# Residual additions merged into the phase that reads their result, chunk by chunk

## The chip, the core and the metric

The kernel runs on one core of one Trainium2 chip. The metric is the device time of one execution in microseconds (us). The core's engines work side by side and meet only at semaphores: PE multiplies matrices (PEld loads its weights), DVE is the vector engine, ACT the scalar engine with its activation functions, POOL a second, slower vector engine, and SP issues most of the DMAs. PE, DVE, ACT and POOL compute on SBUF, PE writes to PSUM.

## The reference

One layer of a hybrid decoder, for 1024 prompt tokens and 8 x 4 sample tokens together (1056 tokens). Cut to what the change touches:

```python
def _rmsnorm(x, g):
    y = x * lax.rsqrt(jnp.mean(x * x, axis=-1, keepdims=True) + NORM_EPS)
    return y * g

f = _swiglu(_rmsnorm(h, ffn1_pre_g), ffn1_wg, ffn1_wu, ffn1_wd)
h = h + 0.5 * _rmsnorm(f, ffn1_post_g)            # r1
u = _rmsnorm(h, mix_pre_g) @ w_in                 # input projection
...                                               # attention, RWKV-7, gates: not touched
h = h + _rmsnorm(mix @ w_out, mix_post_g)         # r2
f = _swiglu(_rmsnorm(h, ffn2_pre_g), ffn2_wg, ffn2_wu, ffn2_wd)
h = h + 0.5 * _rmsnorm(f, ffn2_post_g)            # r3
gp = sigmoid(_rmsnorm(h, ple_pre_g) @ w_ple_gate)
h = h + _rmsnorm(gp * (pemb @ w_ple_proj), ple_post_g)   # r4
```

D_MODEL is 1024, FFN_DIM 2816, everything is float32.

## The kernel before

The stream `x` lies in SBUF channel by channel: 8 chunks (KC) of 128 channels by 1056 tokens (T). PE works on three token blocks of 352 (TB, NTB = 3). The layer is a row of phases, and no engine starts a phase before all have ended the last one: f1 (first feed-forward), r1 (its residual), in (input projection), the middle, merge, r2, f2, r3, pl (per-layer embedding), r4.

**Products.** Each is made of three matmuls on split operands (`mm3`): a float32 value is written as a rounded part `hi` and a rest `lo`. ACT makes `hi`, DVE makes `lo`, for weights and stream alike. A unit is 128 output channels: 8 chunks x 3 blocks x 3 = 72 matmuls. Units of weights come by DMA from the SP queue. A phase begins with `gain_split` (u_hi on ACT, u_lo on DVE, with the first weights between the second and third chunk), and PE's first block of the first unit takes chunk after chunk as u_lo comes (`u_lo_ready`).

**Norms.** The factor 1/rms of a token is applied when a product leaves PSUM. `Norm` makes it in a long chain: ACT squares the chunks, DVE adds them up (`dve_sums`), PE sums over channels with 9 one-column matmuls (`pe_sums`), ACT takes the root, DVE makes the reciprocal (128x9) and a diagonal matrix (`dve_diag`), PE spreads it to all partitions (`pe_spread`), and ACT copies it to `rb` (`act_rb`). In f1, f2 and in, PE does this behind the first or second unit. `NextNorm` takes the squares of a phase's output while its last products run, for the residual behind it (not for r2, which squares for itself).

**Residuals.** `residual_phase` loads all 8 chunks of the old stream in one DMA of 4.2 MB (L699), scales each chunk on DVE out of PSUM (L730), adds the old chunk (L719; even chunks on POOL, odd ones on DVE) and stores the new stream with 8 DMAs. Only then the next phase begins.

**Order.** There is no scheduler: each engine runs its list in the order of the code. Names: `c_x` is x, `f_psg`, `f_psu`, `f_psd` the PSUM tiles of a feed-forward, `in_ps` and `pl_ps` those of in and pl, `n_*` the tiles of a norm, `r_*` of a residual.

Of the kernel before, what the change touches and what calls it, by code (L numbers as in the profile page):

```python
# [213 lines left out]
def gain_split(nc, act, dve, x, g, hi, lo, hi_ready, lo_ready, first_weights, x_in=None):  # L214


    for c in range(x.shape[1]):
        if c == 2:
            first_weights()
        if x_in is not None:  # L220
            x_in(act or dve, c)
        if act is not None:
            act.activation(hi[:, c, :], x[:, c, :], ACT.Copy, scale=g[:, c:c + 1]).then_inc(hi_ready, 1)
        if dve is not None:
            dve.wait_ge(hi_ready, c + 1)
            dve.scalar_tensor_tensor(out=lo[:, c, :], in0=x[:, c, :], scalar=g[:, c:c + 1],
                                     in1=hi[:, c, :], op0=ALU.mult, op1=ALU.subtract).then_inc(lo_ready, 1)


def ffn_phase(nc, env, name, x, g_col, wgu, wd, buf, x_src=None, reading=None):  # L230
# [7 lines left out]
    with Phase(nc) as ctx:  # L238
# [10 lines left out]
        norm = Norm(nc, ctx, name + "n", env, KC, D_MODEL, buf)  # L249
        after = NextNorm(nc, ctx, name, buf)  # L250
        gate, up = norm.sq[:, 0, :], norm.sq[:, 1, :]
# [54 lines left out]
        def x_in(eng, c):  # L306
            if x_src is not None:
                eng.wait_ge(x_loaded[c], 16)

        @block.sync  # L310
        def _(sp):
# [6 lines left out]
            load(0, 0, 0)  # L318
            if x_src is not None:
                for c in range(KC):  # L320
                    sp.dma_start(x[:, c, :], x_src[:, c, :]).then_inc(x_loaded[c], 16)

            def step(s, sv):
                for u in units(s)[1 if sv == 0 else 0:]:
                    load(s, sv, u)
# [14 lines left out]
        def _(act):  # L340
            gain_split(nc, act, None, x, g_col, u_hi, u_lo, u_hi_ready, u_lo_ready,
                       lambda: split_hi(act, 0, 0), x_in)
            norm.act_squares(act, x)
# [11 lines left out]
            def step(s, sv):  # L355
                if sv < NS:
                    for u in (1, 2, 3):
                        split_hi(act, s, u)
# [28 lines left out]
        def _(dve):  # L387
            gain_split(nc, None, dve, x, g_col, u_hi, u_lo, u_hi_ready, u_lo_ready,
                       lambda: split_lo(dve, 0, 0), x_in)
            norm.dve_sums(dve)  # L390
            norm.dve_diag(dve)
            rb3 = norm.rb[:, :].rearrange("p (b t) -> p b t", b=NTB)
# [37 lines left out]
            def step(s, sv):  # L430
                has_up = sv < NS
                last_up = isinstance(s, int) and s == NS - 1
                if has_up:
                    split_lo(dve, s, 1)
                    split_lo(dve, s, 2)
                    gate_evac(s, 0)
                    split_lo(dve, s, 3)
# [14 lines left out]
                if sv > 0:  # L452
                    wait(dve, added, (s - 1) * 24)
                    if sv == 1:
                        dve.wait_ge(u_lo_ready, KC)
                        dve.wait_ge(norm.sq_ready, KC)
                        if reading is not None:
                            dve.wait_ge(*reading)
# [17 lines left out]
        @block.gpsimd  # L476
        def _(pool):
            after.add(pool, range(1, KC - 1))

        @block.tensor  # L480
        def _(pe):
            def up_unit(s, u):
# [3 lines left out]
                for b in range(NTB):  # L486
                    for c in range(KC):
                        if isinstance(s, int) and s == 0 and u == 0 and b == 0:
                            pe.wait_ge(u_lo_ready, c + 1)
# [6 lines left out]
            def step(s, sv):  # L496
                if sv < NS:
                    for u in range(4):
                        up_unit(s, u)
                        if sv == 0 and u == 0:  # L500
                            norm.pe_sums(pe, ps_d[:, 1, :])
                            norm.pe_spread(pe, nbanks)
# [18 lines left out]
class Units:  # L521
# [39 lines left out]
    def product(self, pe, out, k, first, chunks, x_hi, x_lo, tokens, x_ready=None):  # L561


        for c in range(chunks):
            if x_ready is not None:
                pe.wait_ge(x_ready, c + 1)
# [6 lines left out]
def token_block(b):  # L573
    return slice(b * TB, (b + 1) * TB)


def input_projection_phase(nc, env, x, g_col, w_units, proj, buf, reading):


    with Phase(nc) as ctx:  # L580
# [8 lines left out]
        norm = Norm(nc, ctx, "inn", env, KC, D_MODEL, buf)  # L589
# [10 lines left out]
        def _(sp):  # L600
# [5 lines left out]
            for k in range(2):  # L606
                wu.load(sp, 0, k)
            with sp.Fori(1, N_IN // 2) as i:
# [7 lines left out]
            sp.wait_ge(*reading)  # L616

        @block.scalar
        def _(act):
            gain_split(nc, act, None, x, g_col, u_hi, u_lo, u_hi_ready, u_lo_ready,  # L620
                       lambda: wu.split_hi(act, 0, 0))
            wu.split_hi(act, 0, 1)
            norm.act_squares(act, x)
# [7 lines left out]
        def _(dve):  # L631
            gain_split(nc, None, dve, x, g_col, u_hi, u_lo, u_hi_ready, u_lo_ready,
                       lambda: wu.split_lo(dve, 0, 0))
            wu.split_lo(dve, 0, 1)
            norm.dve_sums(dve)
            norm.dve_diag(dve)
            dve.wait_ge(norm.rb_ready, 3)

            def evac(i, k):
# [3 lines left out]
                                  norm.rb[:, :].rearrange("p (b t) -> p b t", b=NTB), ALU.mult)\  # L643
# [14 lines left out]
        def _(pe):  # L658
            def unit(i, k):
                wu.ready(pe, i, k)  # L660
                wait(pe, unit_out, i * 2 + (k - 1))
                for b in range(NTB):
                    mm = wu.product(pe, ps[:, k, b, 0:TB], k, 0, KC, u_hi, u_lo, token_block(b),
                                    u_lo_ready if isinstance(i, int) and i == 0 and k == 0 and b == 0 else None)
                mm.then_inc(wu.used, 1)

            unit(0, 0)
            unit(0, 1)
            norm.pe_sums(pe, psn[:, 1, :])
# [2113 lines left out]
```

## Time and profile before

| what | value |
|---|---|
| median of 3 runs | 3861.78 us (3854.52 to 3871.53) |
| profiled execution: its time | 3863.07 us |
| its span in the profile | 3861.3 us |
| PE busy | 3430.6 us (89%) |
| DVE busy | 1695.9 us (44%) |
| ACT busy | 929.8 us (24%) |
| POOL busy | 440.8 us (11%) |
| granted TensorE clock, mean | 0.932 of 2.4 GHz |

Busy time is time in which an engine has an instruction in work, so 89% of PE does not say that the last 11% is all there is to win; what the engines wait for at the seams between phases is read from the timeline.

### The profile page before, as it was taken

The numbers are of one execution on the slowest core, as the hardware profiler recorded it, in microseconds if no ns is written. First come the engines' busy times: TensorE is split into PE (matmuls) and PEld (weight loads), VectorE is DVE, ScalarE is ACT, GpSimd is POOL, SyncE is SP. The second block draws the span as 40 slices with busy tenths as digits, with TensorE's granted clock in tenths as the row PEclk, the third lists the DMA queues.
The fourth block names the chain that finished last, engine by engine and source line by source line (L and its number), as shares of the span: only waits on it lengthen the run. The fifth ranks groups of instructions, "written<-read, shape, count | busy, mean of one in ns | idle before, by whom it ended". The sixth has DMA issues, their size and how long they took to land. (4 is left out here: it accounts for less than half of the span.)

```text
span 3861.3 us, 69674 instructions
## 1 busy us (share of the span) xinstructions
PE 3430.6 (89%) x28907; PEld 3086.5 (80%) x28907; DVE 1695.9 (44%) x2998; ACT 929.8 (24%) x1610; POOL 440.8 (11%) x457
## 2 busy tenths in 40 slices
PE   7999999969999799889994888869869999999776
PEld 6999999959999637766662767659859999999766
DVE  3343343353121245345444777755154443343443
ACT  3111111121000105434441333333221111111131
POOL 0000000020000000033331344420010000000212
PEclk9999999979999898989996899979979999999878
DMA  2011111122222300056552011023121111111122
GB/s 102 34 55 45 50 39 45 44 107 75 91 94 94 110 2 13 16 206 208 191 192 60 14 31 31 12 95 117 67 83 50 50 50 33 50 50 39 75 80 97
DMA packets 114583, 279.64 MB, mean 72 GB/s; under 512 B 45428, under 2 KB 56500, under 8 KB 113236
## 3 DMA queue, kind: packets, MB, share of 16 engines
q1 hardware_dynamic: 95860, 199.87, 15.4%
q0 software_dynamic: 18432, 75.51, 5.6%
q8 instruction: 229, 3.75, 0.4%
q14 instruction: 62, 0.51, 0.0%
HBM read 231.41 MB, written 43.80 MB: 71 GB/s over the span
## 5 line engine op out<-in xcount | busy, mean ns | idle before, releaser
L79 PE MATMUL f_psg<-f_u_hi,f_w_hi 128*128 128x352 f32 x1056 | 347.1, 329 | 62.7 <-DVE f_w_lo L336 58.2
L428 DVE TENSOR_TENSOR c_x<-c_x,f_psd 128x352 f32<-128x352 f32 x480 | 246.2, 519 | 318.0 <-PE f_psd L81 318.0
L79 PE MATMUL f_psd<-f_hid_hi,f_w_hi 128*128 128x352 f32 x1056 | 350.3, 332 | 18.2 <-DVE c_x L428 9.8
L332 ACT ACTIVATE f_w_hi<-f_raw 128x1024 fp32r<-128x1024 f32 x132 | 136.6, 1054 | 915.7 <-PE f_psd L81 352.3
L79 PE MATMUL f_psu<-f_u_hi,f_w_hi 128*128 128x352 f32 x1056 | 342.5, 324 | 5.5 <-DVE f_w_lo L336 5.5
L80 PE MATMUL f_psg<-f_u_lo,f_w_hi 128*128 128x352 f32 x1056 | 342.7, 325 | 0.0
L81 PE MATMUL f_psg<-f_u_hi,f_w_lo 128*128 128x352 f32 x1056 | 342.5, 324 | 0.0
L80 PE MATMUL f_psd<-f_hid_lo,f_w_hi 128*128 128x352 f32 x1056 | 341.6, 324 | 0.0
L81 PE MATMUL f_psd<-f_hid_hi,f_w_lo 128*128 128x352 f32 x1056 | 341.3, 323 | 0.0
L80 PE MATMUL f_psu<-f_u_lo,f_w_hi 128*128 128x352 f32 x1056 | 340.2, 322 | 0.0
L81 PE MATMUL f_psu<-f_u_hi,f_w_lo 128*128 128x352 f32 x1056 | 339.8, 322 | 0.0
L336 DVE TENSOR_TENSOR f_w_lo<-f_raw,f_w_hi 128x1024 fp32r<-128x1024 f32 x132 | 159.2, 1221 | 353.0 <-ACT f_w_hi L332 353.0
L79 PE MATMUL in_ps<-in_u_hi,inw_hi 128*128 128x352 f32 x864 | 281.5, 326 | 31.3 <-DVE inw_lo L555 30.1
L80 PE MATMUL in_ps<-in_u_lo,inw_hi 128*128 128x352 f32 x864 | 278.8, 323 | 0.0
L81 PE MATMUL in_ps<-in_u_hi,inw_lo 128*128 128x352 f32 x864 | 278.5, 322 | 0.0
L79 PEld LDWEIGHTS f_psg<-f_u_hi,f_w_hi 128*128 128x128 f32 x1056 | 201.5, 191 | 67.5 <-DVE f_w_lo L336 45.6
L118 POOL TENSOR_TENSOR n_total<-n_total,n_sq 128x1056 f32<-128x1056 f32 x18 | 44.4, 2469 | 1735.7 <-ACT n_sq L111 1735.7
L79 PEld LDWEIGHTS f_psd<-f_hid_hi,f_w_hi 128*128 128x128 f32 x1056 | 199.6, 189 | 35.1 <-DVE c_x L428 20.2
L79 PEld LDWEIGHTS f_psu<-f_u_hi,f_w_hi 128*128 128x128 f32 x1056 | 199.5, 189 | 5.8 <-DVE f_w_lo L336 5.8
L80 PEld LDWEIGHTS f_psg<-f_u_lo,f_w_hi 128*128 128x128 f32 x1056 | 202.0, 191 | 0.0
L81 PEld LDWEIGHTS f_psg<-f_u_hi,f_w_lo 128*128 128x128 f32 x1056 | 201.6, 191 | 0.0
L80 PEld LDWEIGHTS f_psd<-f_hid_lo,f_w_hi 128*128 128x128 f32 x1056 | 200.0, 189 | 0.0
(391 smaller groups left out, 7226.3 us busy)
## 6 DMA issues: line engine op xcount, KB each, us to landing
f_raw<-in_ffn_gu SPq DMA_DIRECT2D x88, 512.0 KB, 4.3
f_raw<-in_ffn_d SPq DMA_DIRECT2D x44, 512.0 KB, 4.0
proj<-in_out SPq DMA_DIRECT2D x36, 528.0 KB, 2.9
inw_raw<-in_w_in_units SPq DMA_DIRECT2D x36, 512.0 KB, 3.9
h<-c_x SPq DMA_DIRECT2D x24, 528.0 KB, 2.7
r_old<-h SPq DMA_DIRECT2D x3, 4224.0 KB, 12.9
c_x<-proj SPq DMA_DIRECT2D x16, 528.0 KB, 4.5
mgw_raw<-in_merge_units SPq DMA_DIRECT2D x16, 512.0 KB, 4.7
```

The costliest lines, as they stand in the source:

```text
L79: pe.matmul(out, w_hi, x_hi, start=start, stop=False)
L80: pe.matmul(out, w_hi, x_lo, start=False, stop=False)
L81: return pe.matmul(out, w_lo, x_hi, start=False, stop=stop)
L118: eng.tensor_tensor(total, total, self.buf.sq[:, c % 2, :], ALU.add).then_inc(self.added, 1)
L332: act.activation(w_hi[:, u % 3, :], raw[:, u % 3, :], ACT.Copy).then_inc(hi_done, 1)
L336: dve.tensor_tensor(w_lo[:, u % 3, :], raw[:, u % 3, :], w_hi[:, u % 3, :], ALU.subtract).then_inc(lo_done, 1)
L428: dve.tensor_tensor(a, a, ps_d[:, n % 2, 0:TB], ALU.add).then_inc(added, 1)
```

## The change

The phases r1, r2 and r3 are gone. Their work is done at the head of in, f2 and pl by a class `Residual`; r4 stays as a phase of its own. `Residual` keeps a ring of three old chunks instead of all eight, loads and stores chunk by chunk, and DVE scales chunk c+1 before it splits chunk c. DVE adds chunks 0, 2, 4, 6, 7 and POOL 1, 3, 5 (in pl DVE adds 0, 1, 2, 4, 6, 7). `WideNorm` takes the place of `Norm` in these phases: PE sums the squares of a chunk straight into three rows of PSUM, 32 partitions each, the root and the reciprocal work on 96x352, and a matmul with one row spreads each block. At the head of in, f1, f2 and pl PE takes each chunk for all three blocks at once, the sum of the chunk's squares behind it; the second unit (except in pl) is done in blocks behind the first, and the spread comes behind the second. In pl the products of the embedding come ahead of the chunks.

```diff
+class WideNorm:
+    def act_square(self, act, x, c):
+        wait(act, self.sq_summed, c - 1)
+        act.activation(self.buf.sq[:, c % 2, :], x[:, c, :], ACT.Square).then_inc(self.sq_ready, 1)
+    def pe_sum(self, pe, bank, c):
+        pe.wait_ge(self.sq_ready, c + 1)
+        for b in range(NTB):
+            mm = pe.matmul(bank[32 * b:32 * (b + 1), 0:TB], self.env.ones[:, 0:32],
+                           self.buf.sq[:, c % 2, token_block(b)], start=c == 0, stop=c == KC - 1)
+        mm.then_inc(self.sq_summed, 1)
...
+    def dve_reciprocal(self, dve):
+        dve.wait_ge(self.sd_ready, 1)
+        dve.reciprocal(self.buf.rs[0:self.ROWS, :], self.buf.sd[0:self.ROWS, :]).then_inc(self.rs_ready, 1)
+    def pe_spread(self, pe, banks):
+        pe.wait_ge(self.rs_ready, 1)
+        for b in range(NTB):
+            if b >= len(banks):
+                pe.wait_ge(self.rb_ready, b - len(banks) + 1)
+            pe.matmul(banks[b % len(banks)][:, 0:TB], self.env.ones[32 * b:32 * b + 1, :],
+                      self.buf.rs[32 * b:32 * b + 1, :], start=True, stop=True).then_inc(self.spread, 1)
...
+class Residual:
+    RING = 3
+    def sp_all(self, sp):
+        for c in range(self.RING):
+            self.sp_load(sp, c)
+        for c in range(KC):
+            self.sp_store(sp, c)
+            if c + self.RING < KC:
+                self.sp_load(sp, c + self.RING)
+    def dve_scale(self, dve, c, rb):
+        dve.scalar_tensor_tensor(out=self.x[:, c, :], in0=self.x[:, c, :], scalar=self.gain[:, c:c + 1], in1=rb,
+                                 op0=ALU.mult, op1=ALU.mult).then_inc(self.scaled, 1)
+        if c in self.by_dve:
+            self.add_old(dve, c, self.dve_added)
...
@@ input projection
+            res_norm.act_root(act, psn[:, 1, :])
+            res_norm.act_rb(act, nbanks)
+            wu.split_hi(act, 0, 0)
+            for c in range(KC):
+                res.wait_chunk(act, c)
+                act_hi(act, x, g_col, u_hi, c, u_hi_ready)
+                if c == 0:
+                    wu.split_hi(act, 0, 1)
+                norm.act_square(act, x, c)
...
+            for c in range(KC):
+                pe.wait_ge(u_lo_ready, c + 1)
+                if c == KC - 1:
+                    norm.pe_sum(pe, psn[:, 1, :], c)
+                if c == 0:
+                    wu.ready(pe, 0, 0)
+                for b in range(NTB):
+                    mm = mm3(pe, ps[:, 0, b, 0:TB], ...)
+                if c < KC - 1:
+                    norm.pe_sum(pe, psn[:, 1, :], c)
             unit(0, 1)
-            norm.pe_sums(pe, psn[:, 1, :])
             norm.pe_spread(pe, nbanks)
```

DVE at the seam from f1 to the input projection, before: the residual r1 (`r1_*`), and behind the two branches the input projection's own splits (`in_u_lo`, weights `inw_lo`) and norm (`n1_*`).

```order
L723 TENSOR_SCALAR r1_gain<-c_gains 128x8
L177 RECIPROCAL n1_rs<-n1_sd 128x9
L182 TENSOR_TENSOR n1_diag<-c_ident,n1_rs 128x512 x2
L182 TENSOR_TENSOR n1_diag<-c_ident,n1_rs 128x128
L730 SCALAR_TENSOR_TENSOR c_x1<-c_x1,r1_gain,r1_rb 128x1056 x3
L719 TENSOR_TENSOR c_x1<-c_x1,r1_old 128x1056
L730 SCALAR_TENSOR_TENSOR c_x1<-c_x1,r1_gain,r1_rb 128x1056 x2
```

The same place with the change (`inr_*` is the residual inside the input projection):

```order
L327 TENSOR_SCALAR inr_gain<-c_gains 128x8
L268 RECIPROCAL n1_rs<-n1_sd 96x352
L332 SCALAR_TENSOR_TENSOR c_x1<-c_x1,inr_gain,n1_rb 128x1056
L340 TENSOR_TENSOR c_x1<-c_x1,inr_old 128x1056
L741 TENSOR_TENSOR inw_lo<-inw_raw,inw_hi 128x1024
L332 SCALAR_TENSOR_TENSOR c_x1<-c_x1,inr_gain,n1_rb 128x1056
L359 SCALAR_TENSOR_TENSOR in_u_lo<-c_x1,c_gains,in_u_hi 128x1056
L741 TENSOR_TENSOR inw_lo<-inw_raw,inw_hi 128x1024
L332 SCALAR_TENSOR_TENSOR c_x1<-c_x1,inr_gain,n1_rb 128x1056
L340 TENSOR_TENSOR c_x1<-c_x1,inr_old 128x1056
L359 SCALAR_TENSOR_TENSOR in_u_lo<-c_x1,c_gains,in_u_hi 128x1056
```

The splits of the stream stand between the scalings now; the scaling reads its factor from the SBUF tile `n1_rb`, where it read the PSUM tile `r1_rb`; and the diagonal is gone.

PE at the same seam with the change, from the head of the phase (before, 9 one-column matmuls and a spread of 512, 512 and 32 columns stood in r1, and 72 matmuls of the first unit, block by block, at the head of the input projection):

```order
L257 MATMUL in_psn<-n1_total,c_ones 32x352 x3
L276 MATMUL in_psn<-n1_rs,c_ones 128x352 x3
L79 MATMUL in_ps<-in_u_hi,inw_hi 128x352
L80 MATMUL in_ps<-in_u_lo,inw_hi 128x352
L81 MATMUL in_ps<-in_u_hi,inw_lo 128x352
L79 MATMUL in_ps<-in_u_hi,inw_hi 128x352
L80 MATMUL in_ps<-in_u_lo,inw_hi 128x352
L81 MATMUL in_ps<-in_u_hi,inw_lo 128x352
L79 MATMUL in_ps<-in_u_hi,inw_hi 128x352
L80 MATMUL in_ps<-in_u_lo,inw_hi 128x352
L81 MATMUL in_ps<-in_u_hi,inw_lo 128x352
L251 MATMUL in_psn<-n1_sq,c_ones 32x352 x3
```

Nine matmuls and three sums now stand for each chunk, eight times over.

## Rows read from the trace of the kernel before

**Rows 1.** The page's first line: span of the profiled execution

```profile
span 3861.3 us, 69674 instructions
```

**Rows 2.** Timeline of PE, head of f1: start, duration, instruction, idle before and releaser

```profile
43.89 0.66 PE L79 MATMUL f_psu<-f_u_hi,f_w_hi 128*128 128x352 f32 x1 [2.71 <-DVE f_w_lo L336]
```

**Rows 3.** Timeline of DVE, head of f1: the second unit has ended

```profile
57.98 1.26 DVE L407 TENSOR_TENSOR n_sq<-f_psu,n_rb 128x1056 f32<-128x1056 f32 x1 [10.71 <-PE f_psu L81]
```

**Rows 4.** Timeline of PE, r1 and head of the input projection

```profile
827.37 3.97 PE L166 MATMUL r_sum<-c_ones,n_total 128*128 128x1 f32 x18 [3.79 <-PEq L62]
832.68 4.05 PE L206 MATMUL r_rb<-n_diag,c_ones 128*128 128x512 f32 x6 [1.34 <-DVE n_diag L182]
...
900.14 0.66 PE L79 MATMUL in_ps<-in_u_hi,inw_hi 128*128 128x352 f32 x1 [3.01 <-DVE inw_lo L555]
```

**Rows 5.** Timeline of DVE, r1

```profile
840.23 3.76 DVE L730 SCALAR_TENSOR_TENSOR c_x<-c_x,r_gain,r_rb 128x1056 f32<-128x1056 f32 x3 [6.80 <-DMA r_old<-in_x]
```

**Rows 6.** The tile r_old: from issue to landing

```profile
DMA to landing us min/median/max: 12.6/12.8/13.0
```

**Rows 7.** Costliest groups of the page: busy us, mean ns of one

```profile
L332 ACT ACTIVATE f_w_hi<-f_raw 128x1024 fp32r<-128x1024 f32 x132 | 136.6, 1054 | 915.7 <-PE f_psd L81 352.3
...
L336 DVE TENSOR_TENSOR f_w_lo<-f_raw,f_w_hi 128x1024 fp32r<-128x1024 f32 x132 | 159.2, 1221 | 353.0 <-ACT f_w_hi L332 353.0
```

**Rows 8.** The tile c_x: min/median/max ns of its instructions

```profile
L148 ACT ACTIVATE n_sq<-c_x x35: 1066/1084/1094, 22.7 to 3701.0; 128x1056 f32<-128x1056 f32 x35
L730 DVE SCALAR_TENSOR_TENSOR c_x<-c_x,r_gain,r_rb x32: 1296/1302/1315, 840.2 to 3854.1; 128x1056 f32<-128x1056 f32 x32
...
L830 ACT ACTIVATE c_x<-mg_pso x24: 464/465/466, 2696.7 to 2784.4; 128x352 f32<-128x352 f32 x24
...
L223 ACT ACTIVATE f_u_hi<-c_x,c_gains x16: 1159/1161/1177, 11.5 to 2833.9; 128x1056 fp32r<-128x1056 f32 x16
...
L719 POOL TENSOR_TENSOR c_x<-c_x,r_old x16: 2419/3367/3439, 841.7 to 3853.1; 128x1056 f32<-128x1056 f32 x16
L719 DVE TENSOR_TENSOR c_x<-c_x,r_old x16: 1241/1281/2136, 843.9 to 3855.4; 128x1056 f32<-128x1056 f32 x16
```

**Rows 9.** The tile pl_u_lo, min/median/max ns

```profile
L226 DVE SCALAR_TENSOR_TENSOR pl_u_lo<-c_x,c_gains,pl_u_hi x8: 1305/1306/4752, 3674.3 to 3693.0; 128x1056 fp32r<-128x1056 f32 x8
```

**Rows 10.** Timeline of POOL, head of pl

```profile
3682.40 4.65 POOL L977 TENSOR_TENSOR pl_p_lo<-pl_p,pl_p_hi 128x2112 fp32r<-128x2112 f32 x1 [11.71 <-ACT pl_p_hi L931]
```

**Rows 11.** Timeline of PE in the sample attention: four column strips

```profile
1803.16 0.64 PE L1728 MATMUL sa_ps_o<-sa_pages,sa_weights 128*32 128x256 f32 x8
```

**Rows 12.** The tile n_rs, min/median/max ns

```profile
L177 DVE RECIPROCAL n_rs<-n_sd x8: 215/215/215, 36.1 to 3833.2; 128x9 f32<-128x9 f32 x8
```

**Rows 13.** The line L1314, min/median/max ns

```profile
L1314 DVE RECIPROCAL pa_rinv<-pa_rsum x8: 191/192/203, 1463.0 to 1625.2; 128x8 f32<-128x8 f32 x8
```

**Rows 14.** Windows of f1: busy us (instructions) by engine, granted clock, DMA share, GB/s

```profile
24.00:28.00 4.00, 3.98 (x25) 3.98 (x26) 3.71 (x4) 2.97 (x4) 0.00 (x0) 1.00 0.00 0
...
44.00:48.00 4.00, 4.00 (x14) 4.00 (x15) 3.27 (x3) 2.84 (x3) 0.00 (x0) 0.50 0.00 0
```

**Rows 15.** Timeline of ACT, head of f1: the first chunk is in

```profile
11.51 1.17 ACT L223 ACTIVATE f_u_hi<-c_x,c_gains 128x1056 fp32r<-128x1056 f32 x1 [3.63 <-DMA c_x<-in_x]
```

**Rows 16.** Timeline of ACT, start of r2

```profile
2785.67 1.08 ACT L145 ACTIVATE n_total<-c_x 128x1056 f32<-128x1056 f32 x1 [0.77 <-PEq L62]
```

**Rows 17.** Timeline of DVE, head of f2: the second unit has ended

```profile
2871.27 1.26 DVE L407 TENSOR_TENSOR n_sq<-f_psu,n_rb 128x1056 f32<-128x1056 f32 x1 [9.96 <-PE f_psu L81]
```

**Rows 18.** Timeline of PE, start of r3

```profile
3643.22 3.95 PE L166 MATMUL r_sum<-c_ones,n_total 128*128 128x1 f32 x18 [3.96 <-PEq L62]
```

**Rows 19.** Timeline of DVE in pl: the first unit's last block has ended

```profile
3723.79 0.52 DVE L967 TENSOR_TENSOR pl_gate<-pl_ps,n_rb 128x352 f32<-128x352 f32 x1 [3.19 <-PE pl_ps L81]
```

**Rows 20.** Timeline of PE, start of r4

```profile
3828.86 3.97 PE L166 MATMUL r_sum<-c_ones,n_total 128*128 128x1 f32 x18 [4.93 <-PEq L62]
```

**Rows 21.** Timeline of DVE, r4

```profile
3841.95 3.76 DVE L730 SCALAR_TENSOR_TENSOR c_x<-c_x,r_gain,r_rb 128x1056 f32<-128x1056 f32 x3 [7.04 <-DMA r_old<-h]
```

More of the change, by code:

```diff
@@ L387, in _ @@
         def _(dve):
[L388 to L392, printed above, removed]
+            if res is not None:
+                res.dve_gain(dve)
+                res_norm.dve_reciprocal(dve)
+                dve.wait_ge(res_norm.rb_ready, NTB)
+                res.dve_scale(dve, 0, buf.rb[:, :])
+            split_lo(dve, 0, 0)
+            for c in range(KC):
+                if res is not None and c < KC - 1:
+                    res.dve_scale(dve, c + 1, buf.rb[:, :])
+                x_in(dve, c)
+                dve_lo(dve, x, g_col, u_hi, u_lo, c, u_hi_ready, u_lo_ready)
+                if c == 0:
+                    split_lo(dve, 0, 1)
+            norm.dve_reciprocal(dve)
+            rb3 = buf.rb[:, :].rearrange("p (b t) -> p b t", b=NTB)
             def gate_evac(s, j):
@@ L477, in _ @@
         def _(pool):
+            if res is not None:
+                res.pool_adds(pool)
             after.add(pool, range(1, KC - 1))
@@ L559, in ready, with product @@
         pe.wait_ge(self.lo_done, i * 2 + (k + 1))
-    def product(self, pe, out, k, first, chunks, x_hi, x_lo, tokens, x_ready=None):
+    def product(self, pe, out, k, first, chunks, x_hi, x_lo, tokens):
         for c in range(chunks):
-            if x_ready is not None:
-                pe.wait_ge(x_ready, c + 1)
             w = slice((first + c) * P, (first + c + 1) * P)
@@ L607, in _ @@
                 wu.load(sp, 0, k)
+            res.sp_all(sp)
             with sp.Fori(1, N_IN // 2) as i:
@@ L615, in _ @@
                 sp.wait_ge(stored[k], 16 * (N_IN // 2))
-            sp.wait_ge(*reading)
+            sp.wait_ge(res.stored, 16 * KC)
+        @block.gpsimd
+        def _(pool):
+            res.pool_adds(pool)
         @block.scalar
         def _(act):
[L620 to L623, printed above, removed]
+            res_norm.act_root(act, psn[:, 1, :])
+            res_norm.act_rb(act, nbanks)
+            wu.split_hi(act, 0, 0)
+            for c in range(KC):
+                res.wait_chunk(act, c)
+                act_hi(act, x, g_col, u_hi, c, u_hi_ready)
+                if c == 0:
+                    wu.split_hi(act, 0, 1)
+                norm.act_square(act, x, c)
             norm.act_root(act, psn[:, 1, :])
@@ L631, in _ @@
         def _(dve):
[L632 to L637, printed above, removed]
+            res.dve_gain(dve)
+            res_norm.dve_reciprocal(dve)
+            dve.wait_ge(res_norm.rb_ready, NTB)
+            res.dve_scale(dve, 0, buf.rb[:, :])
+            wu.split_lo(dve, 0, 0)
+            for c in range(KC):
+                if c < KC - 1:
+                    res.dve_scale(dve, c + 1, buf.rb[:, :])
+                res.wait_chunk(dve, c)
+                dve_lo(dve, x, g_col, u_hi, u_lo, c, u_hi_ready, u_lo_ready)
+                if c == 0:
+                    wu.split_lo(dve, 0, 1)
+            norm.dve_reciprocal(dve)
+            dve.wait_ge(norm.rb_ready, NTB)
             def evac(i, k):
@@ L981, in _ @@
         def _(pe):
-            for n in range(KC):
+            res_norm.pe_total(pe, psn[:, 1, :])
+            res_norm.pe_spread(pe, nbanks)
+            wu.ready(pe, 0, 0)
+            pe.wait_ge(p_lo_ready, 1)
+            for b in range(NTB):
+                wu.product(pe, ps[:, b, 1, 0:TB], 0, KC, PC, p_hi, p_lo, token_block(b))
+            for c in range(KC):
+                pe.wait_ge(u_lo_ready, c + 1)
+                if c == KC - 1:
+                    norm.pe_sum(pe, psn[:, 1, :], c)
+                w = slice(c * P, (c + 1) * P)
+                for b in range(NTB):
+                    mm = mm3(pe, ps[:, b, 0, 0:TB], wu.hi[:, 0, w], wu.lo[:, 0, w], u_hi[:, c, token_block(b)],
+                             u_lo[:, c, token_block(b)], c == 0, c == KC - 1)
+                    if c == KC - 1:
+                        mm.then_inc(wu.used, 1)
+                if c < KC - 1:
+                    norm.pe_sum(pe, psn[:, 1, :], c)
+            norm.pe_spread(pe, nbanks)
+            for n in range(1, KC):
                 wu.ready(pe, n // 2, n % 2)
```

298 lines of the change are left out of this document (202 added, 96 removed).

## The prediction, made before the changed kernel ran

> **What bounds the kernel now.** I read the page, then the timeline of each engine at the seams between phases, then single tiles. The span is 3861.3 us [rows 1] and PE is busy through most of it, so a change at the seams can win only what PE waits or idles there; the loops between are untouched. At four seams PE waits for a chain through the other engines. I mark each by two points: its start, and the first moment at which PE goes on with work that the change leaves as it is.
>
> | seam | start | point behind it | length |
> |---|---|---|---|
> | f1 | first chunk in, 11.5 [rows 15] | second unit ended, 57.9 [rows 3] | 46.4 |
> | r1 and in | 827.4 | third unit starts, 900.1 [rows 4] | 72.7 |
> | r2 and f2 | 2785.7 [rows 16] | second unit ended, 2871.2 [rows 17] | 85.5 |
> | r3 and pl | 3643.2 [rows 18] | first unit ended, 3723.7 [rows 19] | 80.5 |
> | r4 | 3828.9 [rows 20] | the end, 3861.3 [rows 1] | 32.4 |
>
> In r1 the scaling starts 12.9 us after the phase, because it waits 6.8 us for the DMA of the old stream [rows 5], which takes 12.8 us to land [rows 6]; r4 shows the same wait of 7.0 us [rows 21].
>
> **Prices.** Behind one another, DVE's operations on 128x1056 follow at 1.25 us each (three in 3.76 [rows 5]), be it scaling, adding or splitting; a weight split costs ACT 1.05 and DVE 1.22 [rows 7]. ACT needs 1.16 for u_hi and 1.08 for a square, 0.47 for 352 columns out of PSUM [rows 8]. A product matmul takes 0.16 us at the high level of the clock (25 in 3.98) and 0.29 at the low one (14 in 4.00) [rows 14]: nine of them 1.4 or 2.6, a whole unit of 72 11.5 us.
>
> The sum of squares has no row. Eight plain float32 matmul instructions of 256 columns in four strips of 32 took 0.64 us in all [rows 11]; with 352 columns that makes 0.9 us for a chunk's three strips, or 1.8 at the low clock. That the strips run side by side is the assumption; one behind the other, three blocks are 1056 plain columns, and 1056 such columns took 4.05 us at the low clock [rows 4], so 2.0 at the high one. I take 0.9. The spread is bounded by the same row: 4.05 for all, 1.35 a block at the low clock. The third block waits for a free bank, so I take first block, copy, third block, copy: 3.9 us at the low clock, 3.0 at the high.
>
> The reciprocal on 352 columns has no row either. Nine columns take 215 ns [rows 12] and eight 191 [rows 13]. Below, it costs per column what the scaling does, 352 of 1056 columns in 1.3 us [rows 8], 0.4 us; above, 24 ns for each further column, the difference of the two rows, makes 8.5 us. The upper end also takes the whole 191 ns of eight columns as their own, with no fixed part, which no engine here shows. So I sit near the lower end: 1.5.
>
> **The port that DVE and POOL share.** This decides the feed. DVE's additions took up to 2136 ns where 1241 is the least; POOL's took 3367 in the median where 2419 is the least [rows 8]. A split of pl took 4752 ns instead of 1306 [rows 9], just while POOL held a 4.65 us operation [rows 10]. But the scaling, which reads its factor from PSUM, never took over 1315 next to POOL [rows 8]. So a DVE instruction with two SBUF operands and a POOL one exclude each other, for a whole instruction. The change moves the factor of the scaling to SBUF, so that now every DVE operation of the feed is of this kind, and POOL's time adds to DVE's instead of hiding.
>
> The Trainium skill says so too ("SBUF — State Buffer", "SBUF: two separate sides"): the pair is an exclusive lock, held for the whole instruction, against a DVE instruction with two SBUF inputs. By that rule the trace agrees; if the two only shared, each feed would be some 7 us shorter and the sum 22 us larger.
>
> **The feed of in and f2.** DVE has 8 scalings, 5 additions, 8 splits and 2 weight splits, 21 x 1.25 + 2 x 1.2 = 28.7 us, and POOL three additions of 2.42 with the port, 7.3. Laid out in order of the code, with ACT's u_hi always done behind other DVE work, the eighth split ends 35.9 us after the first scaling begins. PE needs 2.3 us a chunk at the high clock, 4.4 at the low; the chunks come 4.5 us apart on average, so the feed hides PE. The last two splits are 1.25 apart, so PE ends its chunk 7 two chunks' work later: 2.3 + 2.3 - 1.25 = 3.4 us behind the last split (7.5 at the low clock). Then 11.5 for the second unit.
>
> Behind that something new is exposed: spread (3.0), then ACT splits the next weights (1.05) and DVE (1.22). In f1 and f2 the third unit also needs the gate tile evacuated (1.25), which stood under the second unit before; with handovers 6.2 us from the second unit's end in f1 and f2, and 5.2 in in, where an evacuation runs ahead of the split. PE then starts low, which costs 13 matmuls x 0.13, some 2 us; before, that was paid at the start of the second unit in f1 [rows 2] and within it in f2, and in in both pay it.
>
> **Seam by seam.** *in*: column sum 1.8, root 0.6, reciprocal 1.5, spread 3.9 are 7.8, then 35.9, 3.4, 11.5, 5.2: 63.8 against 72.7, 8.9 less. With part of the tail at the low clock I take 8. The first old chunk is no wait: two weight loads and it, 1.6 MB, against 4.2 MB in 12.8 us [rows 6]; each later load is issued two to three chunks ahead, although it stands behind a store on SP. The next unit's weights stand behind the last store, still 11 us ahead of their use.
>
> *f2*: the squares with their sums take 12.3 (eight at ACT's 1.08 behind some slow ones at 1.8), root 0.6, reciprocal 1.5, spread 3.7, then 35.9, 3.4, 11.5, 6.2: 75.1 against 85.5, less 2 for the low clock, 8.4; I take 7.5.
>
> *pl*: 7.8 to the scaling. The feed has one addition more on DVE, one less on POOL, but POOL's 4.65 us operation takes the port behind the first addition: laid out, 38.5. PE then needs 2.0 to the sum of chunk 7, root 0.6, reciprocal 1.5, spread 3.0, weights 1.3 and 1.5, first gate, sigmoid and product 1.7: 57.9 to the second unit's start, against 80.5, less 2 for the clock, 20.6. It is so much because two of three blocks of the first unit, 60 matmuls at 0.16, and the whole of the norm's additions ran exposed before. I take 19.5.
>
> *f1*: no residual. ACT sets the pace, 2.15 to 2.24 a chunk, PE 2.3: the eight chunks end at about 34.7, the second unit at 46.2, the third starts at 52.4, low (2): 54.4 against 57.9, 3.5.
>
> *r4*: 1.8, 0.6, 1.5 and a spread of some 2 with three banks: scaling starts 5.9 after the phase instead of 13.1 [rows 20, 21], less 0.7 for a fifth addition on DVE (1.25, part of it a wait for POOL before): 6.
>
> **Sum:** 3.5 + 8 + 7.5 + 19.5 + 6 = 44.5 us. The profiled execution took 3863.1, so 3818.6; the median of the runs shown lies 1.3 below it, and I write 3818.
>
> **The rivals.** *(a) As laid out*, gains of 30 to 60 us: 0.72.
>
> *(b) The reciprocal is long.* Five of the eight are exposed (first ones of in, f2, pl, the second of pl, r4); the others lie under the second unit. At 3 us the sum falls by 7.5, to 3826; at 8.5 us by 35, to a gain of 9, 3853. The narrow rows speak for less, their slope for more. The Trainium skill ("VectorE: DVE Perf Modes", "Walkthrough: the 8-slice pipeline in each mode") has the reciprocal as an iterative divide with a repeat count of 8; as an estimate from its 0.96 GHz that is 2.9 us for 352 columns, the first of these two cases. No run here shows it yet. Gains of 9 to 30 by this or by smaller mishaps of the kind: 0.17.
>
> *(c) The transfers or the port bind less*: POOL's additions slip into DVE's gaps, the clock stays high. Gains over 60, 3795: 0.04.
>
> *(d) Slower.* The column sums run one behind another and PE stays at the low clock through the feed: 4.05 + 2.6 = 6.7 us a chunk. Then PE, not DVE, sets the pace: 6 to the first chunk and 53.6, against 35.9 + 3.4, is 20 more at three seams, and 14 + 53.6 against 34.7 is 33 more in f1; 94 in all, so 49 slower, 3911. It decides from a pace of 5.2 us a chunk on. The row of strips speaks against it, and dense work brings the clock up. 0.04. That the old and new versions are the same within the measurement by yet other ways: 0.03.
>
> **How the numbers follow.** A measurement of this kernel tells about 0.5%, 19 us, from no change. Faster by more: (a), (c) and most of (b), 0.89. Same: the rest of (b) and the odd cases, 0.07. Slower 0.04. The range takes (a) with the unknown prices: the clock at the tails (12 us), the reciprocal (7), the sums (6), to both sides: 3798 to 3840.
>
> **What the profile will show.** L332 begins about 8 us behind the phase's first column sum and takes over 2 us where a POOL addition runs; eight u_lo within 36 to 38 us; L251 three at a time within a microsecond; the reciprocal at 0.5 to 3 us; PE idle 5 to 6 us behind the second unit. If L251 takes over 2 us a chunk at the high clock, or u_lo comes in under 30 us, I am wrong in a step.

## The result, and the profile after

The changed kernel takes 3814.56 us (median of 4 runs, 3812.72 to 3827.01), the kernel before 3860.45 (4 runs beside it). The ratio is 0.9885, with a 95% interval from 0.9854 to 0.9915: 46 us or 1.2% less. Forecast were 3818, a range of 3798 to 3840, and "faster" with 0.89. The profiled execution took 3814.7 us; its page begins:

```profile
span 3812.9 us, 69816 instructions
```

against 3861.3 [rows 1]. To see where the 48.4 us between the two spans come from, I cut both at ten moments that the change leaves alone, each a row's start in the timeline of DVE, PE or ACT: DVE's second gate evacuation of f1 (the third unit has ended), f1's last product, DVE's third and last evacuation of the input projection, ACT's last copy out of the merge, the same two points of f2, DVE's fourth gate tile of pl, pl's last product, the end. The lengths between, worked out from the starts:

```
stretch           before    after   before - after   forecast
f1 seam            69.43    65.03        4.40           3.5
f1, the rest      753.83   756.92       -3.09           0
in seam            91.31    82.92        8.39           8
in, the rest      377.64   384.90       -7.26           0
middle           1492.23  1483.45        8.78           0
f2 seam            98.28    89.40        8.88           7.5
f2, the rest      756.23   751.63        4.60           0
pl seam            89.65    70.87       18.78          19.5
pl, the rest       95.02    96.88       -1.86           0
r4                 37.63    30.89        6.74           6
```

The five seams give 47.2 us, where 44.5 were forecast. "The rest" rows are the surprise: untouched loops that move by up to 9 us. One execution of each kernel is cut here. Two more profiles of the old kernel's code (e6 and e12 below, which only pad) gave 68.3 and 70.2 us for the f1 seam, 94.8 and 89.5 for in, 98.3 and 97.7 for f2, 89.9 and 89.6 for pl, so the single figure of in is good to a few us, the others to 1 or 2.

DVE's timeline at the head of the input projection, after (start, duration, instruction, idle before and releaser), stands against [rows 5]:

```profile
826.05 0.17 DVE L327 TENSOR_SCALAR inr_gain<-c_gains 128x8 f32<-128x8 f32 x1 [0.81 <-PEq L62]
827.94 2.35 DVE L268 RECIPROCAL n_rs<-n_sd 96x352 f32<-96x352 f32 x1 [1.72 <-ACT n_sd L263]
834.50 1.32 DVE L332 SCALAR_TENSOR_TENSOR c_x<-c_x,inr_gain,n_rb 128x1056 f32<-128x1056 f32 x1 [4.21 <-ACT n_rb L282]
...
839.46 1.31 DVE L359 SCALAR_TENSOR_TENSOR in_u_lo<-c_x,c_gains,in_u_hi 128x1056 fp32r<-128x1056 f32 x1
840.69 3.46 DVE L741 TENSOR_TENSOR inw_lo<-inw_raw,inw_hi 128x1024 fp32r<-128x1024 f32 x1
...
849.12 1.31 DVE L359 SCALAR_TENSOR_TENSOR in_u_lo<-c_x,c_gains,in_u_hi 128x1056 fp32r<-128x1056 f32 x1
850.35 3.48 DVE L332 SCALAR_TENSOR_TENSOR c_x<-c_x,inr_gain,n_rb 128x1056 f32<-128x1056 f32 x1
...
856.34 1.31 DVE L332 SCALAR_TENSOR_TENSOR c_x<-c_x,inr_gain,n_rb 128x1056 f32<-128x1056 f32 x1
857.57 1.31 DVE L359 SCALAR_TENSOR_TENSOR in_u_lo<-c_x,c_gains,in_u_hi 128x1056 fp32r<-128x1056 f32 x1
858.80 3.50 DVE L332 SCALAR_TENSOR_TENSOR c_x<-c_x,inr_gain,n_rb 128x1056 f32<-128x1056 f32 x1
...
867.41 2.71 DVE L359 SCALAR_TENSOR_TENSOR in_u_lo<-c_x,c_gains,in_u_hi 128x1056 fp32r<-128x1056 f32 x2
```

and POOL's, in the same stretch:

```profile
839.70 3.38 POOL L340 TENSOR_TENSOR c_x<-c_x,inr_old 128x1056 f32<-128x1056 f32 x1 [16.10 <-DVE c_x L332]
849.36 3.37 POOL L340 TENSOR_TENSOR c_x<-c_x,inr_old 128x1056 f32<-128x1056 f32 x1 [6.28 <-DVE c_x L332]
857.80 3.39 POOL L340 TENSOR_TENSOR c_x<-c_x,inr_old 128x1056 f32<-128x1056 f32 x1 [5.08 <-DVE c_x L332]
```

Each of the three POOL additions has one DVE instruction beside it that takes 3.5 us instead of 1.2 to 1.3, be it a scaling or the split of the weights. The feed, from the first scaling's start at 834.50 to the eighth split's end at 867.41 + 2.71 = 870.12, takes 35.6 us; 35.9 were laid out. No DVE row waits for an old chunk any more. PE at the end of three seams, against [rows 3, 4, 17]:

```profile
52.01 0.63 PE L79 MATMUL f_psg<-f_u_hi,f_w_hi 128*128 128x352 f32 x1 [4.02 <-DVE n_sq L562]
...
891.47 0.66 PE L79 MATMUL in_ps<-in_u_hi,inw_hi 128*128 128x352 f32 x1 [3.06 <-DVE inw_lo L741]
...
2841.96 0.32 PE L81 MATMUL f_psu<-f_u_hi,f_w_lo 128*128 128x352 f32 x1
2842.21 0.86 PE L276 MATMUL f_psd<-n_rs,c_ones 1*128 1x352 f32 x4
2843.62 0.85 PE L276 MATMUL f_psd<-n_rs,c_ones 1*128 1x352 f32 x2 [0.55 <-ACT n_rb L282]
2848.49 0.63 PE L79 MATMUL f_psg<-f_u_hi,f_w_hi 128*128 128x352 f32 x1 [4.02 <-DVE n_sq L562]
```

Behind f2's second unit the spread and 4.02 us of idle time stand exposed, 6.3 us from the spread's start to the third unit (6.2 forecast).

### The profile page after: what moved, and what is told of

Its sections match the earlier page's. It is cut to its first block and busy times, and to the rows that moved or that the text cites. A ratio compares the mean times of both kernels' runs of the same rounds, so it can differ in the third digit from the quotient of the medians.

```text
span 3812.9 us, 69816 instructions
## 1 busy us (share of the span) xinstructions
PE 3439.1 (90%) x29021; PEld 3073.2 (81%) x29021; DVE 1679.0 (44%) x2939; ACT 935.1 (25%) x1619; POOL 428.7 (11%) x452
## 3 DMA queue, kind: packets, MB, share of 16 engines
q1 hardware_dynamic: 99892, 199.87, 15.7%
## 5 line engine op out<-in xcount | busy, mean ns | idle before, releaser
L79 PE MATMUL in_ps<-in_u_hi,inw_hi 128*128 128x352 f32 x864 | 285.2, 330 | 17.6 <-DVE in_u_lo L359 14.5
L118 POOL TENSOR_TENSOR n_total<-n_total,n_sq 128x1056 f32<-128x1056 f32 x18 | 44.5, 2474 | 1701.6 <-ACT n_sq L111 1701.6
L81 PEld LDWEIGHTS f_psd<-f_hid_hi,f_w_lo 128*128 128x128 f32 x1056 | 200.2, 190 | 0.0
```

Of the source, the lines that this page charges most:

```text
L79: pe.matmul(out, w_hi, x_hi, start=start, stop=False)
L81: return pe.matmul(out, w_lo, x_hi, start=False, stop=stop)
L118: eng.tensor_tensor(total, total, self.buf.sq[:, c % 2, :], ALU.add).then_inc(self.added, 1)
```

## The experiments

Twelve kernels ran. The executions of one kernel spread by 9 to 21 us, so small effects are read from the stretches. Where the code is the same, the f1 seam came out at 65.0 to 66.9 us, the middle at 1483 to 1497 and f2's rest at 744 to 757.

```
seam     before  after    e1     e2     e3     e4     e7     e8     e9    e11
f1        69.43  65.03  66.63  66.58  59.85  75.75  59.75  66.90  59.70  69.78
in        91.31  82.92  81.05  78.17  78.01  92.75  72.10  87.23  71.95  86.67
f2        98.28  89.40  86.06  83.78  83.81  99.70  78.16  92.62  78.17  93.19
pl        89.65  70.87  68.43  70.56  70.91  79.16  68.75  75.43  68.69  79.07
r4        37.63  30.89  30.69  30.89  30.89  30.88  30.88  33.26  30.88  30.86
```

**e1: no addition on POOL,** in in, f2 and pl.

```
-        res, res_norm = Residual(nc, ctx, "inr", x, *old, (0, 2, 4, 6, 7)), ...
+        res, res_norm = Residual(nc, ctx, "inr", x, *old, tuple(range(KC))), ...
```

> All eight residual additions of the in, f2 and pl feeds on DVE, none on POOL; nothing else is changed. My theory, that a POOL operation and a DVE operation with two SBUF operands exclude each other: three POOL additions of 2.42 us leave the port and three DVE additions of 1.25 come, 3.5 us less in in and in f2 (from the first scaling to the eighth split 32.1 us instead of 35.6), and with two additions 2.3 us less in pl (36.0 instead of 38.3). Together some 9 us less, 3805. Rival, that POOL's additions are hidden and DVE's are the pace: 3.75 us more in in and f2, 2.5 more in pl, 10 us more, 3824, with feeds of 39.4 and 40.8 us.

Measured 3815.03 us (4 runs), ratio 0.9875 [0.9853, 0.9898]. The feeds took 33.5, 33.1 and 36.7 us, and the seams fell by 1.9, 3.3 and 2.4. The rival, feeds of 39.4, is out; my 32.1 was too low by two things: POOL had held DVE up by 2.2 us each time (3.48 less 1.31) and not 2.42, and a scaling whose own addition follows on DVE passes on 0.2 us later than one before other work (834.50 to 835.92 against 856.34 to 857.57 in after). The whole time doesn't show the 7.6 us: in the profiled execution, middle and f2's rest came out 12 us longer than in that of after.

**e2: the factor of the scaling from PSUM.**

```
-            res_norm.act_rb(act, nbanks)
...
-            res_norm.pe_spread(pe, nbanks)
+            res_norm.pe_spread(pe, [ps[:, 1, b, :] for b in range(NTB)])
-                    res.dve_scale(dve, c + 1, buf.rb[:, :])
+                    res.dve_scale(dve, c + 1, ps[:, 1, :, 0:TB])
```

> In in and f2 the scaling reads its factor from three PSUM banks, into which the spread goes, instead of from SBUF; the copies of the residual's factor by ACT are gone; pl stays. My theory: the first scaling begins 1.7 us earlier after the reciprocal (2.5 us behind it instead of 4.2), and the scaling is no longer locked out by POOL (L332 never much over 1.3 us beside an L340 of POOL), so that up to 1.3 of each of three POOL additions hides: between 3.4 and 11 us less over both seams, I take 8, 3806. Rival, that POOL's time only falls on the next split or addition: L332 is 1.3 but the feed stays 35.6 us, and 3.4 us are won, 3811.

Measured 3806.33 us (4 runs), ratio 0.9867 [0.9843, 0.9891]. DVE, a stretch of in that begins with the reciprocal:

```profile
830.37 2.35 DVE L268 RECIPROCAL n_rs<-n_sd 96x352 f32<-96x352 f32 x1 [1.84 <-ACT n_sd L263]
834.44 1.31 DVE L333 SCALAR_TENSOR_TENSOR c_x<-c_x,inr_gain,in_ps 128x1056 f32<-128x1056 f32 x1 [1.71 <-PE in_ps L276]
...
850.26 1.31 DVE L333 SCALAR_TENSOR_TENSOR c_x<-c_x,inr_gain,in_ps 128x1056 f32<-128x1056 f32 x1
851.67 2.09 DVE L341 TENSOR_TENSOR c_x<-c_x,inr_old 128x1056 f32<-128x1056 f32 x1
```

while POOL holds

```profile
849.26 3.38 POOL L341 TENSOR_TENSOR c_x<-c_x,inr_old 128x1056 f32<-128x1056 f32 x1 [6.27 <-DVE c_x L333]
```

The scaling at 850.26 runs in 1.31 beside POOL, and the addition behind it, with two SBUF operands, waits out the remainder. So only a DVE instruction with two SBUF operands is locked out, and a part of POOL's time, 0.7 us of each addition, hides under the PSUM scaling: the feeds are 33.4 and 33.5 us, 2.1 less. The rival, an unchanged 35.6, is out, though what is left of POOL's time does fall on the next addition, as it said. The idle time ahead of the first scaling went from 4.21 to 1.71. The two seams fell by 4.8 and 5.6.

**e3: the spread within the second unit.**

```
-                up_unit(0, 1)
-                norm.pe_spread(pe, nbanks)
+                up_unit(0, 1, [lambda: norm.pe_spread(pe, nbanks, (0, 1)), lambda: norm.pe_spread(pe, nbanks, (2,))])
...
                 for b in range(NTB):
                     ...
+                    if b < len(behind):
+                        behind[b]()
```

> The spread of the following norm stands behind the first and the second token block of the second unit (two blocks of it, then one) instead of behind the whole unit, in f1, f2 and in. My theory: root, reciprocal, copies, the weight splits and the first evacuation then run under the unit. PE's idle time ahead of the third unit, 4.0 us in f1 and f2 and 3.1 in in, goes, and with it the low clock behind it, some 2 us each: 15 to 18 us less, 3798. Rival, that the wait is one for the weights or moves on to the next unit: under 5 us less, 3811 or more.

Measured 3807.26 us (4 runs), ratio 0.9852 [0.9829, 0.9875]. The seams of f1, in and f2 fell by 5.2, 4.9 and 5.6, 15.7 together, as the theory had it. The median lies only 7.3 us below that of after and missed the 3798. In the profiled execution the middle was 14 us longer than in after, which hides the gain there; four executions from 3798.36 to 3812.04 don't settle more. e7 and e9 below bring it in full. PE around the start of f1's third unit, windows (length, busy us and instructions, granted clock, DMA share, GB/s), after and then e3:

```profile
42.00:46.00 4.00, 4.00 (x26) 1.00 0.00 0
46.00:50.00 4.00, 1.45 (x6) 0.75 0.00 0
50.00:54.00 4.00, 1.99 (x7) 0.50 0.02 5
```

```profile
44.00:48.00 4.00, 4.00 (x25) 1.00 0.00 0
48.00:52.00 4.00, 4.00 (x25) 1.00 0.49 129
52.00:56.00 4.00, 4.00 (x28) 1.00 0.70 254
```

With the gap, the low level (0.50) that followed it goes too.

**e4: the first unit whole.**

```
                     norm.pe_sum(pe, ps_d[:, 1, :], c)
-                    for b in range(NTB):
-                        mm = mm3(pe, ps_g[:, b, 0:TB], w_hi[:, 0, w], ..., u_hi[:, c, token_block(b)], ...)
+                up_unit(0, 0)
                 up_unit(0, 1)
```

> The feed of one unit chunk by chunk is undone in f1, in, f2 and pl: the column sums still come with the chunks, but the first unit runs by token blocks when all eight chunks are split, as before; the residual stays in the following stage. My theory: the tail of PE behind the last split becomes a whole unit, 11.5 us instead of 3.4, so 8 us more in in and f2, 9 in f1, and 6 in pl, where part of the norm then hides under the unit: 31 us more, 3845, which leaves 14 us to the moved residual. Rival, that most of the gain is the moved residual (the wait for the old chunks and the scaling under the feed) and the low clock in a sparse feed eats what the chunk feed wins: under 12 us more, 3826.

Measured 3860.68 us (11 runs), ratio 1.0001 [0.9989, 1.0013]: the time of the kernel before. Against after, the seams grew by 10.7, 9.8, 10.3 and 8.3, 39 us, not 31, and the whole time by 46, so that both 3845 and the rival's 3826 missed; the other 7 lie in the untouched stretches, within their spread. DVE's last splits and PE behind them in in:

```profile
875.40 2.72 DVE L359 SCALAR_TENSOR_TENSOR in_u_lo<-c_x,c_gains,in_u_hi 128x1056 fp32r<-128x1056 f32 x2
```

```profile
872.94 1.40 PE L251 MATMUL in_psn<-n_sq,c_ones 128*32 128x352 f32 x6 [4.59 <-DVE in_u_lo L359]
876.76 2.80 PE L251 MATMUL in_psn<-n_sq,c_ones 128*32 128x352 f32 x12 [2.43 <-DVE in_u_lo L359]
879.49 0.66 PE L79 MATMUL in_ps<-in_u_hi,inw_hi 128*128 128x352 f32 x1
879.95 0.49 PE L80 MATMUL in_ps<-in_u_lo,inw_hi 128*128 128x352 f32 x1
```

Here the last sums and the unit's first matmuls run at the low level (the window 876 to 880 was granted 0.50), which my 8 us for the tail had left out. That the moved residual brings nothing would be the wrong reading, as e11 shows.

**e5 and e6: where the weight tiles begin.** The changed kernel and e1 to e4 take exactly 384.90 us in the rest of in, and 96.9 in that of pl; a single PE matmul takes some 3 ns more. Their `inw_hi`, `inw_lo`, `plw_hi` and `plw_lo` begin 32 bytes behind a multiple of 64, since the residual's 128x8 tile of gains, 32 bytes a partition, stands ahead of them. In f2 it stands behind the weights. Before, all of them began on a multiple of 256.

```
+        sb("pad", [P, KC], F32)          # e5, in and pl of the kernel after
         wu = Units(nc, ctx, "inw", w_units, KC * P)
```

```
+        sb("pad", [P, 8])                # e6, in and pl of the kernel before
         wu = Units(nc, ctx, "inw", w_units, KC * P)
```

> The changed kernel with 32 bytes of unused memory per partition ahead of the weight tiles of in and pl, so that they begin on a multiple of 64 bytes, as before the change; with the change they began 32 bytes behind one, because of the 32-byte tile of gains. Nothing else moves. My theory: this start is why the untouched loop of in (third unit's end to the last evacuation) takes 384.9 us in every kernel with the change and 377.6 before, and the untouched part of pl 96.9 instead of 95.0. Then they are back at 377.6 and 95.0, and 9 us are won, 3805. Rival, that the cadence comes from another thing of the change (the order of tiles, the larger buffers, what DMA does): 384.9 and 96.9 stay, 3814.

> The kernel before with 32 bytes of unused memory ahead of the weight tiles of in and pl, which then begin 32 bytes behind a multiple of 64; nothing else. My theory: its loop of in goes from 377.6 to 384.9 us and the later part of pl from 95.0 to 96.9, 9 us more, 3868. Rival: 377.6 and 95.0 stay, 3859.

e5: 3812.2 us (4 runs), ratio 0.9882 [0.9866, 0.9897]; e6: 3867.81 (9 runs), ratio 1.0022 [1.0012, 1.0032]. e6 turns the untouched loops of the old kernel into those of the new one, 384.92 and 96.87. e5 brings only part back, 380.50 and 95.60, and both of its expectations missed: its tiles begin 64 bytes behind a multiple of 128, which isn't yet where they were before.

**e9, e10 and e12: which multiple, and which operand.** e9 pads by 224 bytes in in and 96 in pl, e12 is the kernel before with 128 bytes more, e10 moves the other operand:

```
+        sb("pad_u", [P, 8])              # e10, with pad [P, 16] ahead of the weights
         u_hi, u_lo = sb("u_hi", [P, KC, T], F32R), sb("u_lo", [P, KC, T], F32R)
```

> The combined kernel, with the weight tiles of in and pl at a multiple of 128 bytes (in in one that is none of 256, in pl at a multiple of 256) instead of 64 bytes behind one. So far the untouched loop of in took 377.6 us where the tiles began at a multiple of 256 (before), 380.5 where they began 64 bytes behind a multiple of 128, and 384.9 where they began 32 bytes behind one; in pl 95.0, 95.6, 96.9. My theory, that a start on a multiple of 128 is what the fast level wants: 377.6 and 95.0 in both phases, 3.5 us less than the combined kernel, 3775. Rivals: 256 is what it wants, then pl is at 95.0 and in not at 377.6; or it hangs on where the tiles lie to the others, then neither moves.

> The combined kernel, with the weight tiles of in and pl at a multiple of 256 bytes, and the other operand of the products, the split stream (u_hi and u_lo, in pl also p_hi and p_lo), 32 bytes behind a multiple of 128. My theory, that only the start of the stationary weights counts: 377.6 and 95.0 us, 3775. Rival, that any operand of a matmul off the multiple costs the same: 384.9 and 96.9 us, 3784.

> A control: the kernel before with 128 bytes of unused memory ahead of the weight tiles of in and pl. Theory that a multiple of 128 is what counts: 377.6 and 95.0 us as before, no change of the time, 3859. It also gives a third profile of the untouched stretches in the old kernel. The loops of f1 and f2 and the middle took 754, 756 and 1492 us in the profile before and 754, 756 and 1495 in the shifted one, 754, 752 and 1489 in the mean of eleven kernels with the change. If the 8 us between these belong to the change, f2's loop is at 756 and the middle at 1492 or above here too; if they are chance, one of the two falls below 752 or 1489.

```
tiles of in / pl begin                        in, rest  pl, rest  run
weights 0 mod 256, streams 0 mod 128            377.64    95.02   before
weights 128 mod 256 in in, 0 in pl              377.64    95.02   e9
weights 0 mod 128                               377.64    95.02   e12
weights 64 mod 128                              380.50    95.60   e5
weights 32 mod 64                               384.90    96.88   after
weights 0 mod 256, streams 32 mod 128           380.06    95.64   e10
```

A window of 200 us in the loop shows it as a count of matmuls; first the kernel after, then e9:

```profile
1000.00:1200.00 200.00, 200.00 (x1237) 1.00 0.27 93
```

```profile
1000.00:1200.00 200.00, 200.00 (x1260) 1.00 0.28 96
```

A multiple of 128 is enough for the fast level. Both of e10's expectations missed: the moving operand seems to count too, but 32 bytes off cost it 2.4 us and not 7.3. e10's pad also moves the tiles that lie between the stream and the weights (the output tile and the ring of old chunks in in), and no run separates these. The times: e9 below, e10 3781.52 (4 runs), ratio 0.9796 [0.9782, 0.981], e12 3858.47 (10 runs), ratio 1.0001 [0.9989, 1.0014]. e12's middle was 1487.5 us and f2's rest 753.4, so in the middle the old kernel reaches the lower values too. By the mark set ahead (one of the two below 1489 or 752), the 8 us that these stretches seemed to owe to the change are chance. With three profiles of the old kernel a share of a few us isn't excluded.

**e8: each reciprocal twice.**

```
+        dve.wait_ge(self.rs_ready, 1)
+        dve.reciprocal(self.buf.rs[0:self.ROWS, :], self.buf.sd[0:self.ROWS, :]).then_inc(self.rs_ready, 1)
...
-        pe.wait_ge(self.rs_ready, 1)
+        pe.wait_ge(self.rs_ready, 2)
```

> The changed kernel with each of the eight reciprocals done twice, 2.35 us and a handover more each. My theory, that five are on the path (the first of in, of f2, both of pl, that of r4) and three (f1, the second of in and of f2) lie under the second unit: 12 us more, 3827, in the stretches 2.4 more in in and f2, 4.8 in pl, 2.4 in r4 and none in f1. Rival, that all eight are exposed: 19 us more, 3834; or that others hide too, as in pl under the first unit: under 8 us.

Measured 3831.05 us (5 runs), ratio 0.9921 [0.9907, 0.9934], 16.5 us above after, between the 12 of the theory and the 19 of the rival, so the whole time doesn't decide. The seams grew by 4.3, 3.2, 4.6 and 2.4 in in, f2, pl and r4, 14.5, where five times 2.4 make 12. f1's 1.9 lies within the spread of that stretch. The 1.9 too much in in is not a further reciprocal: the second pair there ends at 879.24, and PE's second unit goes on to 887.1. It is clock. Of it, 1.0 arose between the eighth split and the second unit's end, where the window 872 to 876 was granted 0.84 in e8 and 1.00 in after, and 0.8 behind the gap, where 894 to 898 was granted 0.60 and 0.94. Five are on the path.

**e7 and e9, all together.** The edits of e2 and e3, pl's additions on DVE, and weight tiles 64 bytes off (e7) or on a multiple of 128 (e9).

> Four edits at once on the changed kernel: weight tiles at multiples of 64 bytes; the scaling of in and f2 reads its factor from PSUM; pl's additions all on DVE; the spread of the following norm behind the first and second token block of the second unit in f1, in and f2. If the gains add: 9.1 for the tiles, 4.8 and 5.6 for the PSUM factor (by the two stretches of that run), 2.4 for pl, 5.2 and 4.9 and 5.6 for the early spread: 37.6 us less, 3777. Rival, that the edits share one wait, so that the second unit's end is not moved by what is won ahead of it: half of the 26 us at the seams stays, 3790 or more.

e7: 3778.42 us (5 runs), ratio 0.979 [0.977, 0.981]. e9: 3776.55 (5 runs), ratio 0.9789 [0.9776, 0.9802], 82 us below the kernel before and 38 below the change. The gains add: 5.3, 10.8, 11.2 and 2.1 at the four seams.

**e11: the residual alone,** e4 with the early spread and the weight tiles on a multiple of 128.

> The residual moved, without the feed by chunks (the first unit whole, behind all eight splits), and without the two costs that the changed kernel carries: the spread early, within the second unit, and the weight tiles at a multiple of 128 bytes. My theory, that the run with the whole unit came out at the time of before because the residual's 24 us were eaten by 9 us of tile placement and 15 of exposed spread: 3836. Rival, that the moved residual alone is worth little and those costs hide in this order: 3850 or more.

Measured 3831.2 us (6 runs), ratio 0.994 [0.9927, 0.9952]. Its seams against before: f1 0.4 more, in 4.6, f2 5.1, pl 10.6 and r4 6.8 less, 26.7 in all. In e4 the exposed spread (18.6 over the three seams) and the tiles (9.1) had eaten just that, and the rival's 3850 is out. The 26.7 are not all the moved residual: r4, which is no part of the move, has the shorter norm, and its scaling no longer waits for the old stream (it starts 6.2 us behind the phase instead of 13.1). What the move, the shorter norm and the loads by chunks are worth each, no run tells.

## Why the prediction was right

**The cause** was rival (a), as laid out. The gain has two parts, and e4 and e11 price them: the first unit fed by chunks 39 us, the moved residual with the shorter norm 27 (r4's 6.8 included), less 9 for the tiles and some 19 for the late spread, 38 net; the remaining 8 of the 46 measured are within the spread of untouched stretches. The 39 hold for a feed put back where the spread is late, as in e4.

**The port** was right, and it decided the feed: 35.6, 35.6 and 38.3 us against 35.9, 35.9 and 38.5. e1 and e2 take the lock away in two ways and win about 2 us of feed each time. The rule of the Trainium skill ("SBUF — State Buffer", "SBUF: two separate sides") is borne out in the part that e2 tests: a scaling with one operand in PSUM took 1.30 to 1.31 us beside POOL.

**The reciprocal** is the term I mis-sized. All eight rows are alike:

```profile
L268 DVE RECIPROCAL n_rs<-n_sd x8: 2348/2349/2350, 33.4 to 3789.3; 96x352 f32<-96x352 f32 x8
```

2.35 us, not 1.5. The row of nine columns [rows 12] contains a fixed part after all, but the price per column lies far above that of an addition. Five on the path make 4.2 us of error. The estimate of 2.9 us from the repeat count of 8 in the Trainium skill ("VectorE: DVE Perf Modes", "Walkthrough: the 8-slice pipeline in each mode") was nearer than mine and still 0.55 too long. By these rows it is (2349 - 215) / 343 = 6.2 ns a column, five times the scaling's 1.2 at my lower end, and a quarter of the 24 that the slope between [rows 12] and [rows 13] gave, whose 8.5 us was the worse guide. Neither end was near; sitting close to the lower one did the less harm.

**The column sums** were near the mark. Two chunks in the feed of in, the first in a window granted 0.50 (848 to 852), the other in one granted 1.00 (856 to 860); then r4's, at the low level, and the spread behind them:

```profile
850.97 1.40 PE L251 MATMUL in_psn<-n_sq,c_ones 128*32 128x352 f32 x6
858.13 0.79 PE L251 MATMUL in_psn<-n_sq,c_ones 128*32 128x352 f32 x6
...
3787.32 1.39 PE L257 MATMUL r_sum<-n_total,c_ones 128*32 128x352 f32 x6 [5.00 <-PEq L62]
3791.75 1.55 PE L276 MATMUL r_rb<-n_rs,c_ones 1*128 1x352 f32 x6 [3.04 <-DVE n_rs L268]
```

A chunk's three took 0.79 and 1.40 us against 0.9 and 1.8, and r4's spread 1.55 against "some 2". What paid for the reciprocal differs by seam. In in nothing ahead of the third unit did: the first scaling began 8.5 us behind the phase's first column sum instead of 7.8, and the third unit 65.4 (826.04 to 891.47) instead of 63.8 and some 0.9 for the clock, 7.3 us less than the 72.8 before. The seam's 8.4 holds another 1.0 us by the clock, for which the forecast had no term: from its start to its evacuation the third unit took 13.4 us, and 14.4 before. In f2 the squares with their sums did: the reciprocal began 10.7 us behind the phase instead of 12.9. In pl, with two reciprocals exposed, the seam gave 18.8 instead of 19.5. Rival (d), 6.7 us a chunk and PE as the pace, had no place: three times within the feed of in PE waits for a split, 2.87, 1.21 and 3.58 us, at either level of the clock.

Of the signs named ahead, three were off a little: PE stood idle for 3.6 us behind the second unit in in and 4.6 in f1 and f2, not 5 to 6; two of in's three POOL additions held up a scaling and the third a weight split; and in and f2 had their eight splits in 35.6 us, not 36 to 38.

**What I had wrong** is that "the loops between are untouched". Their code is; their tiles were moved by 32 bytes. That cost 9.1 us, a fifth of the gain, and it lay in the diff, as a tile of eight columns allocated ahead of the weights. That the total still came out within 4 us of the forecast is in part luck: the seams gave 2.7 us more than forecast, the tiles took 9.1, and the other untouched stretches gave 10.3 in the profiled pair, which by e12 is chance for all that these runs can tell.

## What to carry to other kernels

When a norm's factor is needed only behind a block of work, issue its spread inside that block as soon as the sums can be ready, since a chain that ends just behind the block costs its whole length and the low clock after it (15.7 us over three seams in e3). Feed a product chunk by chunk wherever another engine makes its operand: here that was the larger part of the gain. An edit that measures as nothing may hold two effects that cancel: the moved residual without the feed came out at the time of before (e4), and at 27 us less once the late spread and the shifted tiles were taken away (e11). After an edit that adds or resizes a tile, compare the length of the loops that the edit leaves alone; a difference that comes back to a hundredth of a microsecond in kernel after kernel is no noise. Here it was placement, and a pad ahead of the weights (56 columns in in, 24 in pl) took it back.

## What was not expected of the hardware

The placement in SBUF of a matmul's operands sets its pace: weights (128x128, four bytes) that begin on a multiple of 128 bytes let the loop of in run in 377.64 us, 64 bytes off in 380.50, 32 bytes off in 384.90, and the moving operand (with the tiles between) 32 bytes off in 380.06, each to 0.02 us where it was repeated. Why, no run shows. A DVE instruction that needs the result of the one just before it on DVE starts 0.2 us later than one that doesn't (1.42 against 1.23 us from a scaling's start to the next instruction's). The kind of instruction isn't the reason: in r4 of the changed kernel an addition follows the scaling of another chunk, and it starts 2.45 us after the first of two scalings, 1.23 for each. Nor is it the scaling's factor in SBUF, since in e2, with the factor in PSUM, the same step takes 1.41 (850.26 to 851.67). The rows of r4:

```profile
3793.48 2.54 DVE L940 SCALAR_TENSOR_TENSOR c_x<-c_x,r_gain,r_rb 128x1056 f32<-128x1056 f32 x2 [1.79 <-PE r_rb L276]
3795.93 1.25 DVE L930 TENSOR_TENSOR c_x<-c_x,r_old 128x1056 f32<-128x1056 f32 x1
```
